# Routing table of a sparse expert layer: built on TensorE from one-hot products instead of by indirect DMAs, with the shared expert's down products placed behind the expert loops

## The reference, cut to what matters

```python
def moe_ffn(h, router_w, router_b, e_gate, e_up, e_down, s_gate, s_up, s_down):
    scores = jax.nn.sigmoid((h @ router_w).astype(jnp.float32))
    _, idx = lax.top_k(scores + router_b.astype(jnp.float32), TOP_K)      # 6 of 64 experts
    w = jnp.take_along_axis(scores, idx, axis=-1)
    w = (w / jnp.sum(w, axis=-1, keepdims=True) * ROUTED_SCALE).astype(h.dtype)
    return routed_experts(h, idx, w, e_gate, e_up, e_down) + swiglu(h, s_gate, s_up, s_down)

def swiglu(h, w_gate, w_up, w_down):                                      # 1024 -> 256 -> 1024
    return (jax.nn.silu(h @ w_gate) * (h @ w_up)) @ w_down
```

## Time and profile before

| what | us |
|---|---|
| median of 3 runs (2589.39 to 2595.86) | 2593.86 |
| the profiled execution's own time | 2595.89 |
| its span, first to last instruction | 2594.0 |
| PE busy in it | 2305.9 |
| DVE / ACT / POOL busy in it | 842.9 / 606.9 / 448.4 |
| mean granted TensorE clock | 0.958 of full |

### The profile page before, as it was taken

How to read it: one execution, slowest core, us unless ns; L and a number is a source line. 1 busy time by engine, 2 the same in 40 slices (tenths; PEclk the granted TensorE clock), 3 DMA queues, 4 the chain that set the end, 5 groups by cost and what they waited for, 6 DMA issues and landing times.

```text
span 2594.0 us, 36647 instructions
## 1 busy us (share of the span) xinstructions
PE 2305.9 (89%) x13212; PEld 1246.4 (48%) x13212; DVE 842.9 (32%) x1699; ACT 606.9 (23%) x1200; POOL 448.4 (17%) x690
## 2 busy tenths in 40 slices
PE   5998899985679999999998799989868999999995
PEld 2463354542245555555554654344334555555555
DVE  3295665144011111111111657663341111111115
ACT  4312354030111212121212142242201211111111
POOL 0000000004123232323232000000033222222220
PEclk8999999997789999999999999999988999999998
DMA  7510000051689999999994712000147999999986
GB/s 321 222 70 33 1 1 1 33 214 63 234 314 407 411 394 398 405 403 398 395 398 187 289 49 86 0 1 17 65 154 306 425 419 415 408 397 390 396 319 229
DMA packets 106818, 626.86 MB, mean 242 GB/s; under 512 B 24346, under 2 KB 28698, under 8 KB 61920
## 3 DMA queue, kind: packets, MB, share of 16 engines
q1 hardware_dynamic: 71888, 556.69, 53.8%
q0 software_dynamic: 33424, 64.04, 6.5%
q10 hardware_dynamic: 1440, 5.24, 0.5%
HBM read 609.49 MB, written 61.92 MB: 259 GB/s over the span
## 4 chain that ended last, share of the span: by engine, by line
PE 67%; DMA 16%; DVE 6%; issue 6%; ACT 2%; another core or an unknown queue 1%; SPq 1%; POOL 0%; POOLq 0%; DVEq 0%; ACTq 0%
PE psum L965 22%; PE psum L625 17%; DMA arena<-in_experts 11%; PE psum L985 10%; PE psum L948 3%; PE psum L792 2%; DMA arena<-y 2%; PE psum L816 2%; PE psum L832 2%; DVE arena L1412 2%; PE psum L704 2%; DMA arena<-in_mod_w 2%; PE psum L618 2%; PE psum L730 1%; PE psum L973 1%
## 5 line engine op out<-in xcount | busy, mean ns | idle before, releaser
L965 PE MATMUL psum<-arena 128*64 128x256 f32 x6272 | 726.7, 385 | 29.5 <-DMA arena<-in_experts 27.5
L965 PEld LDWEIGHTS psum<-arena 128*64 128x64 f32 x6272 | 444.6, 138 | 248.0 <-issue 36.6
L625 PE MATMUL psum<-arena 128*128 128x512 f32 (+1 forms) x1360 | 512.7, 535 | 21.5 <-ACT arena L1080 13.1
L625 PEld LDWEIGHTS psum<-arena 128*128 128x128 f32 x1360 | 261.7, 195 | 268.3 <-issue 240.7
L985 PE MATMUL psum<-arena 128*64 128x512 f32 x1568 | 375.2, 598 | 0.9 <-ACT arena L1317 0.9
L1906 POOL DMA_INDIRECT y<-arena,SIX x196 | 197.8, 1009 | 798.2 <-ACT arena L1317 758.8
L1786 DVE TENSOR_TENSOR arena<-psum,arena 128x128 f32<-128x128 f32 x196 | 57.2, 292 | 748.3 <-ACT arena L1310 708.3
L1310 ACT ACTIVATE arena<-psum 128x128 f32<-128x128 f32 x196 | 54.5, 278 | 654.6 <-PE psum L965 654.6
L1317 ACT ACTIVATE arena<-psum,SIX 128x512 f32<-128x512 f32 x196 | 134.9, 688 | 275.5 <-PE psum L985 266.8
L985 PEld LDWEIGHTS psum<-arena 128*64 128x64 f32 x1568 | 106.0, 136 | 141.4 <-issue 128.2
L1875 POOL DMA_INDIRECT table<-PAY,dsti x60 | 58.3, 972 | 583.7 <-DVE dsti L1756 566.0
(11 more groups left out here) (231 smaller groups left out, 1880.6 us busy)
## 6 DMA issues: line engine op xcount, KB each, us to landing
arena<-in_experts SPq DMA_DIRECT2D x138, 2048.0 KB, 8.9
arena<-in_experts SPq DMA_DIRECT2D x138, 1024.0 KB
arena<-in_mod_w SPq DMA_DIRECT2D x48, 1024.0 KB, 14.0
arena<-y SPq DMA_DIRECT2D x20, 1536.0 KB, 16.8
arena<-in_wblk SPq DMA_DIRECT2D x22, 1024.0 KB, 4.8
arena<-in_shared SPq DMA_DIRECT2D x2, 3072.0 KB, 10.2
hrows<-arena ACTq DMA_DIRECT2D x10, 512.0 KB
y<-arena,SIX POOLq DMA_INDIRECT x196
```

The costliest lines, as they stand in the source:

```text
L625: last = mm(job(l, key, n, parts), a, b, start=i == 0, stop=i == len(pairs) - 1)
L965: last = mm(psum[j * ROWS:(j + 1) * ROWS, s % 2, 0:2 * P], HT[:, s // 2, k, h:h + ROWS], w[:, k * 512 + j * 256:k * 512 + (j + 1) * 256], ...
```

## The change

The DRAM tables, the 60 indirect scatters and the load of the table are gone. For each tile of tokens DVE builds two one-hot arrays from `dsti`: `LO1` (row within 128: 6 x 128 elements) and `HI1` (column among 112, times a code that holds token and choice: 6 x 112), and PE multiplies them, six products per tile (`oh`; `tab` is the last tile), all accumulated in PSUM bank 6. DVE decodes the sum into `TAB`; `swap` is a product that exchanges the two halves of the partitions for the scatter's entries. The `oh` of tile t stands behind the `hr` of tile t + 3, and DVE has two pairs of buffers, so from tile 2 on it waits for the `oh` of two tiles before (`tab_mm`).

The `sd` products move behind the expert loop. Their weights are copied to `WDN` by ACT at `tab`, which frees `WB[2]` (`down_kept`). The strip table `DTAB` of the next layer, whose place the shared hidden values keep until then, is loaded after the last chunk of `y6d`. The expert weights of a token are kept in `WTS` and applied in the combine: ACT scales choices 0 to 2 (`weighted_rows`), DVE multiplies and adds 3 to 5. `y6d` gets 1024 token places per choice in both layers (768 and 512 before), so a token's rows of two choices lie 4 MB apart (3 and 2 MB before). In the shared stage jobs take six banks in turn.

```diff
-                self.shared += [("hr", t, i) for t in range(t_out) for i in range(2)]
-            for m in range(KC):
-                self.shared.append(("sd", m, s))
-                tiles(1)
+                for t in range(t_out):
+                    self.shared += [("hr", t, i) for i in range(2)]
+                    if t >= 3:
+                        self.shared.append(("oh", t - 3))
+                self.shared += [("oh", t) for t in range(t_out - 3, t_out - 1)] + ["tab"]
+                tiles(2)
+                self.shared.append("swap")
+            tiles(2 if s == 0 else len(beside))
...
         self.before_experts = len(j)
+        j += [(("sd", m, s), "D") for s in sq for m in range(KC)]
...
-        y6d = [nc.dram_tensor(f"y6_{l}", (TOPK * plans[l].t_out * P * 2, 512), F32, kind="Internal").ap() for l in range(LAYERS)]
-        tabd = [nc.dram_tensor(f"table{l}", (ROWS * SUBS, 4), I32, kind="Internal").ap() for l in range(LAYERS)]
+        y6d = [nc.dram_tensor(f"y6_{l}", (TOPK * STRIDE * 2, 512), F32, kind="Internal").ap() for l in range(LAYERS)]
...
-            for l in range(LAYERS):
-                sp.dma_start(tabd[l].rearrange("(p b) w -> p b w", p=ROWS), A["blank"].rearrange("(p b) w -> p b w", p=ROWS)
-                             ).then_inc(sem("tab_init"), 16)
...
-                        ready(sp, l, ("sd", KC - 1, pl.sq[-1]))
+                        ready(sp, l, ("su", 1, pl.sq[-1]))
+                        sp.wait_ge(sem("down_kept"), l + 1)
...
+                if l + 1 < LAYERS:
+                    ready(sp, l, ("sd", KC - 1, pl.sq[-1]))
+                    sp.dma_start(DTAB, A["dtab"]).then_inc(sem("dtab_in"), 16)
...
+                    elif st[0] == "oh" or st == "tab":
+                        t = T - 1 if st == "tab" else st[1]
+                        if t == 0:
+                            start_job("tab")
+                        pe.wait_ge(sem("onehot"), 6 * l + t + 1)
+                        for k in range(TOPK):
+                            last = mm(job(l, "tab", SUBS // 2), LO1[t % 2][:, k, :], HI1[t % 2][:, k, :],
+                                      start=t == k == 0, stop=t == T - 1 and k == TOPK - 1)
+                        last.then_inc(done if st == "tab" else sem("tab_mm"), 1)
+                    elif st == "swap":
+                        evacuated(pe, l, "tab")
+                        start_job(st)
+                        for h in range(2):
+                            last = mm(job(l, st, SUBS // 2)[h * ROWS:(h + 1) * ROWS], ident[:, (1 - h) * ROWS:(2 - h) * ROWS],
+                                      TF, start=True, stop=True)
+                        last.then_inc(done, 1)
...
-                    elif st[0] == "sd":
-                        shared_down(st[1], st[2])
...
+                for s in pl.sq:
+                    for m in range(KC):
+                        shared_down(m, s)
...
+                    elif st == "tab":
+                        ready(act, l, st)
+                        act.wait_ge(sem("shared_in"), 16 * (l + 1))
+                        for k in range(FE // P):
+                            last = f(WDN[:, k, :], WB[2][:, WGU + k * D:WGU + (k + 1) * D], ACT.Copy)
+                        last.then_inc(sem("down_kept"), 1)
...
-                    f(YB[:, s, :], psum[:, 3 + s % 2, :], ACT.Copy, scale=SIX[:, s, 2:3].bitcast(F32)
-                      ).then_inc(sem(f"y_a{l}"), 1)
+                    f(YB[:, s, :], psum[:, 3 + s % 2, :], ACT.Copy).then_inc(sem(f"y_a{l}"), 1)
...
+
+                    for i in range(2):
+                        act.wait_ge(sem(f"y6in{t % 3}{i}"), 16 * (t // 3 + 1 + 2 * l))
+                        for k in range(3):
+                            y = Y6[:, t % 3, k, i * 512:(i + 1) * 512]
+                            last = f(y, y, ACT.Copy, scale=WTS[:, t, k:k + 1])
+                        last.then_inc(sem(f"y_scaled{l}"), 1)
...
-                    V.tensor_copy(dsti[:, t, 0:TOPK], rt[:, t, 3, 0:TOPK]).then_inc(sem(f"dest{l}"), 1)
-
-                for s in pl.sq:
+                    link(V.tensor_copy(dsti[:, t, 0:TOPK], rt[:, t, 3, 0:TOPK]))
+                    V.tensor_scalar(LOHI[:, 0, :], dsti[:, t, 0:TOPK], P - 1, None, ALU.bitwise_and)
+                    link(V.tensor_scalar(LOHI[:, 1, :], dsti[:, t, 0:TOPK], 7, None, ALU.arith_shift_right))
+                    if t >= 2:
+                        dve.wait_ge(sem("tab_mm"), 5 * l + t - 1)
+                    hi = HI1[t % 2]
+
+                    def spread(x, n):
+
+                        return x.unsqueeze(2).to_broadcast([P, TOPK, n])
+
+                    V.tensor_tensor(LO1[t % 2], c("iota128").unsqueeze(1).to_broadcast([P, TOPK, P]), spread(LOHI[:, 0, :], P), ALU.is_equal)
+                    link(V.tensor_tensor(hi, c("iota128")[:, 0:SUBS // 2].unsqueeze(1).to_broadcast([P, TOPK, SUBS // 2]),
+                                         spread(LOHI[:, 1, :], SUBS // 2), ALU.is_equal))
+                    V.tensor_tensor(hi, hi, spread(c("code")[:, t * TOPK:(t + 1) * TOPK], SUBS // 2), ALU.mult
+                                    ).then_inc(sem("onehot"), 1)
+                ready(dve, l, "tab")
+                V.tensor_copy(TF, job(l, "tab", SUBS // 2)).then_inc(evacD, 1)
+                evacuated(dve, l, "tab")
+                link(V.tensor_scalar(TI[:, 0, :], TF, c("half"), None, ALU.add))
+                V.tensor_scalar(TABJ[:, :, 0, 3], TI[:, 0, :], 1, STRIDE - 1, ALU.arith_shift_right, ALU.bitwise_and
...
+                ready(dve, l, "swap")
+                link(V.tensor_scalar(TI[:, 1, :], job(l, "swap", SUBS // 2), c("half"), None, ALU.add))
+                for h in range(2):
+                    last = entries(h, 1 - h, TI[:, 1, :])
+                last.then_inc(evacD, 1)
+                evacuated(dve, l, "swap")
+                dve.sem_inc(sem(f"tab_ready{l}"), 1)
...
-                dve.wait_ge(sem("tab_in"), 32 * (l + 1))
-                V.tensor_copy(TAB[ROWS:P, :, 1], TAB[ROWS:P, :, 3]).then_inc(sem(f"tab_ready{l}"), 1)
-                dve.wait_ge(sem(f"tab_ready{l}"), 1)
-                for h in range(2):
-                    pair = TAB[h * ROWS:(h + 1) * ROWS, :, :].rearrange("p (b h) w -> p b h w", h=2)
-                    V.tensor_copy(pair[:, :, 0, 3], pair[:, :, h, 0]).then_inc(sem(f"tab_ready{l}"), 1)
...
                     for i in range(2):
                         dve.wait_ge(sem(f"y6in{t % 3}{i}"), 16 * (t // 3 + 1 + 2 * l))
                         y = Y6[:, t % 3, :, i * 512:(i + 1) * 512]
-                        V.tensor_tensor(y[:, 0:3, :], y[:, 0:3, :], y[:, 3:6, :], ALU.add).then_inc(sem(f"ysum{l}"), 1)
+                        dve.wait_ge(sem(f"y_scaled{l}"), 2 * t + i + 1)
+                        for k in range(3):
+                            last = V.scalar_tensor_tensor(y[:, k, :], y[:, k + 3, :], WTS[:, t, k + 3:k + 4], y[:, k, :], ALU.mult, ALU.add)
+                        last.then_inc(sem(f"ysum{l}"), 1)
+
+                for m in range(KC):
+                    shared_added(m, 0)
+                sums(0)
+                for s in pl.sq[1:]:
+                    for m in range(KC):
+                        shared_added(m, s)
+                for t in range(T):
+                    if t:
...
-                pool.wait_ge(sem("tab_init"), 32)
-                for t in range(T):
-                    pool.wait_ge(sem(f"dest{l}"), t + 1)
-                    for k in range(TOPK):
-                        g.indirect_dma_start(tabd[l], offsets(dsti[:, t, k:k + 1]), PAY[:, t, k, :], None,
-                                             bounds_check=ROWS * SUBS - 1, oob_is_err=False).then_inc(sem("rows_out"), 16)
...
-                for h in range(2):
-                    g.dma_start(TAB[h * ROWS:(h + 1) * ROWS, :, :], tabd[l].rearrange("(p b) w -> p b w", p=ROWS)
-                                ).then_inc(sem("tab_in"), 16)
...
-                pool.wait_ge(sem(f"tab_ready{l}"), 3)
+                pool.wait_ge(sem(f"tab_ready{l}"), 1)
```

95 lines of the change are left out of this document (56 added, 39 removed).

## The result

The changed kernel takes 2553.75 us (median of 4 runs, 2548.63 to 2555.35) against 2594.64 for the kernel before, run beside it; the ratio is 0.9842, 95% interval 0.983 to 0.9853. That is 41 us less, where 56 were forecast; the forecast time was 2538, its range 2515 to 2575. The profiled execution spans 2553.5 us, own time 2555.35.

What follows compares the result with a forecast made beforehand. Bound taken: low-traffic stretches before both expert loops, layer 0's stall from scatters, layer 1's late table. Terms -47.5 - 15.4 - 1 + 4 + 5 - 0.7 = -55.6 gave 2540.3, or 2538 against the median; range 2515 to 2575.

Steps and rivals of the forecast that it cites:

- The stall and its cause: Layer 0's shared stage: ACT's 30.78 us idle read as caused by POOL's 36 scatters, at least 40 us, to 652.
- the second rival: Layer 0: the stall was not the scatters'; ACT or PE stands still some 25 us again, 2563 us; 15%.
- Layer 0, forecast -47.5: Layer 0's shared stage: table summed at 645.6, experts start at 695.7 instead of 743.15; bounds -53 to -42.
- the nine tiles behind it: Layer 0, loads after tile 14: 2.6 us of bandwidth each, three buffers in turn, tile 23 used at 691.7.
- third rival: Layer 0: expert 0 ahead of tile 14, loads fill the gap as before; -35, about 2550 to 2566; 9%.
- Layer 1, forecast -15.4: Layer 1's shared stage: POOL takes its first index at 1930.2 instead of 1945.64; bounds -13 and -19.
- PE is there in time: Layer 1's shared stage: DVE's one-hot work runs without waiting for PE, to 1922.3; table at 1926.3.
- The combines, forecast +4 and +5: Combines of layers 0 and 1: weights and moved products add 4 us (+2 to +8) and 5 us (+3 to +9).
- Loops -1: Both expert loops: only the last two blocks of each gain from ACT's shorter copy, 1 us together.
- start -0.7: Kernel start: `PAY` and the blank tables no longer compete with the first loads; 0.7 us less (0 to -2).
- 4 MB rows: Combine chunk loads: forecast 4 us apart still; rival of slow reads at 4 MB, +76 us, 2614; 8%.
- The rule of the Trainium skill: Combine loads: large power-of-two row pitches lose rate, 103 GB/s at 4 MiB against 207 at 512 KiB; trace disagreed so far.

Runs made afterwards that it cites:

- e5: Kernel before the change, POOL waiting for the token rows' landing ahead of its 36 (24) scatters instead of behind them: 2595.52 us against 2593.45, ratio 1.0011.
- e11: Changed kernel plus 36 tiny scatters in layer 0, all behind the last one-hot columns, pieces 3584 bytes apart: 2582.55 us.
- e12: Changed kernel plus 36 tiny scatters in layer 0, all behind the last one-hot columns, pieces side by side: 2582.63 us.
- e6: Changed kernel plus 36 tiny scatters beside layer 0's stage, to the old kernel's row numbers (pieces 3584 bytes apart): 2562.86 us.
- e7: Changed kernel with SP asking for modulation tiles 14 to 16 ahead of expert 0 instead of behind it: 2546.40 us, ratio to before 0.9831.
- e9: Changed kernel, tiles 14 to 16 ahead of expert 0, expert 2 asked for after the first gather, weights on the product's diagonal: 2535.25 us, ratio to before 0.9782.
- e4: Changed kernel with the routing weights left out of the combine: 2573.45 us, with layer 1's tokens sent to other experts and a round more.
- e1: Changed kernel plus 36 tiny indirect scatters beside layer 0's stage, into a table nobody reads: 2552.61 us.
- e2: Changed kernel plus 36 plain POOL transfers of 128 16-byte pieces at fixed addresses in layer 0: 2553.07 us.

## Why the prediction was right, and where it was not

- **The stall and its cause.** Read as the scatters' from a gap marked "issue" and one marked "remote"; e5, e11 and e12 show it, e6 shows that a pause of POOL ends it. My reckoning that the scatters end with the gap at 652 was off: they stand 1.27 us apart, so they ran until 657.8, ACT acted once among them and stood still again. The nine indirect DMAs behind the table (650.92 to 668.2 in the changed kernel) bring no such gap, so the second rival didn't come. The mechanism below (semaphore events or instructions that don't get through) stays open: no view names it. Two lines of before on that second halt:

```profile
656.80 0.97 POOL L1875 DMA_INDIRECT table<-PAY,dsti  x1 [0.31 <-issue]
660.82 0.60 ACT L1289 ACTIVATE arena<-psum 128x512 f32<-128x512 f32 x1 [7.81 <-remote]
```

- **Layer 0, forecast -47.5, measured -41.0.** The step up to the table held: first wait of DVE until 629.7 (forecast 628), last one-hot products at 645.0 (643.6). The start was 1.6 us later, and the last six products took 2.91 us where I took 2, so SP asked for expert 0 at 650.6 instead of 647.6. Tile 14 came 15.1 us behind that (14.4 forecast). The term that was mis-sized is the nine tiles behind it: 33.0 us to the end of tile 23 (665.74 to 698.74) against 29.7. I had them at 2.6 us of bandwidth with buffers following one another; the trace shows the engines at half their rate from 670 to 686, while the buffers waited for PE, and e7 and e9 show that another order saves 10 and 6 us. The `md` and `mt` behind tile 23 took 4.9 where I had 4. My own third rival, expert 0 ahead of tile 14, was a good part of the truth. Expert 1 was asked for 4.7 us ahead of the first block (698.95), and loop 0 is no longer for it.
- **Layer 1, forecast -15.4, measured -11.5.** POOL's first index came 15.1 us sooner against the picks, as worked out, but not quite by the path that I gave: "PE is there in time" was wrong, DVE waited 3.14 us for the first one-hot products, and the table was decoded 24.5 us behind the first pick where I had 22.0. It cost nothing only because the token rows landed at that same moment (24.2 forecast). What I left out is what comes behind it: SP asks for expert 2 at that very moment, and the gather takes 9.9 us instead of 6.3. e9 gives it back.
- **The combines, forecast +4 and +5, measured +5.4 and +6.6.** Right in kind. In layer 0 the part behind the last chunk is 2.4 us longer, as forecast (1.9 and 0.5); the rest is that chunk's landing 3.0 us later, of which 1.8 stand already at the first chunk. In layer 1 the weights alone are 6.6 (e4), not the products that hold DVE.
- **Loops -1, start -0.7.** Loop 0 0.0. Loop 1 -6.8 is no gain of the change: before's second profile has 573.8, the changed kernel's 573.1. The start's 0.7 is not to be seen where the first column lies between 606.4 and 614.1.
- **Between the layers**, forecast nothing, measured +5.3: the clock, last section. That it, the start and loop 1 cancel (+1.6, +5.3, -6.8) is chance; without it the gain would read 46 us or 34.
- **4 MB rows** cost nothing once the loads run: 3.97 us a chunk in layer 0, 4.06 in layer 1 (2500.66 to 2504.72). Their start is another matter, which I had overlooked: from 2 to 6 us behind the first request layer 0 moves 304 and 240 GB/s at 4 MB where it moved 364 and 399 at 3 MB (windows of 2 us), and layer 1 before the change, at 2 MB, 316 and 236. That is the 2.3 us by which the first chunk takes longer. No run changes the distance alone, so that it is the cause is not shown. The rule of the Trainium skill (DMA: Bandwidth & Descriptors, "Latency and other measured facts") is measured for the distance from one partition's row to the next; in these copies that is 4 KB, so the prediction had no ground to apply it to the distance between choices, and its 103 GB/s at 4 MiB doesn't show.

**What stays open.** On the chip of e1 to e4 (each chip served one batch of runs, so chip and hour can't be told apart) the kernel before took 2550.0 us, and the changed kernel with 36 more scatters (e1) 2552.6, with no stall in its trace. That before has no stall there either is argued from its time and its mean clock (0.960 to 0.966, elsewhere 0.952 to 0.959), not shown. If so, the change gains nothing on that chip, where the changed kernel by itself was not run: without the stall the earlier table and the moved products would be paid back by the weights. The gain of 41 us is then that of the other chips on which the kernel before was timed. Whether plain tiny writes stall the engines like indirect ones is open too (e2).

## To carry to other kernels

Look at what a helper engine does while others stand still without a releaser: 36 indirect scatters of 16-byte rows took 46 us of POOL, moved 74 KB and cost the stage some 30 us; the table by one-hot products takes some 25 us of DVE (six tiles of 4.2, of which 1.25 each were there before) and 12 us of PE. When a stall is taken away, look at once at the order of the queues behind it: here three tiles behind an expert cost 6 to 10 us, and a load issued 0.85 us ahead of a gather 5. Measure on more than one chip before a gain is called the program's.

## What the runs showed of the hardware that was not expected

- While tiny indirect scatters run back to back, a finished product is seen by ACT 41 us late (657.8 to 698.69 in e11), and PE issues one product in 2.1 us; SP asks for a load 35 us late. It begins behind 9 to 19 of them (ACT at 657.8 and PE at 670 in e11, whose first is at 646.44); in e11 the last wait marked "remote" ends 11 us behind the last scatter (DVE at 703.20), in e6 2 us into a pause. In e1, on another chip, it is not there.
- Code that is the same word for word took 425.9 to 426.1 us in four profiles and 428.1 to 431.9 in ten between the layers, by where TensorE's clock fell. Over that stretch of before and of the changed kernel PE is busy 384.19 us and 389.83 us with all but the same count of instructions (1342 and 1343). Windows (start:end, length, busy time and count of PE, PEld, DVE, ACT, POOL, then the granted clock) on the same operations of before and of the changed kernel:

```profile
1621.00:1630.00 9.00, 6.62 (x16) 2.31 (x16) 7.33 (x8) 2.89 (x4) 0.00 (x0) 1.00 0.00 0
```

```profile
1586.00:1598.00 12.00, 9.12 (x18) 3.43 (x20) 7.59 (x8) 3.28 (x4) 0.00 (x0) 0.78 0.01 1
```

In the second the granted clock is at its lower level (1.2 GHz) for part of the window, and the eight products at its start take 6.02 us instead of 3.70. In the 9 us ahead PE did the same 14 instructions in both, busy 5.77 us in before and 6.19 in the changed kernel; there the clock had fallen within that window already (granted 0.91 against 1.00).
